# First layer's values with the input as the stationary operand, for two head pairs at a time, in a two-layer attention trunk

## What is computed

```python
qkv = (rms_norm(x, g0) @ w_qkv).reshape(s, 3, 16, 64)     # q, k, v
z = q @ k.T / 8                                           # per head
log_stay = where(strict, log_sigmoid(-z), 0)              # strict: key before query
log_a = log_sigmoid(z) + cumsum_from_right(log_stay shifted by one)
a = where(strict, exp(log_a), 0)
o = (a @ v) @ w_o
x = x + rms_norm(o, g1)
x = x + rms_norm(swiglu(rms_norm(x, g2), w_gate_up, w_down), g3)
```

## Time and profile before

| | |
|---|---|
| median of 3 runs | 778.37 us (777.60 to 779.53) |
| profiled execution, its own time | 777.7 us |
| its span | 775.8 us |
| TensorE matmul busy | 765.2 us, 99% of the span |
| VectorE busy | 507.3 us, 65% |
| ScalarE busy | 398.3 us, 51% |
| TensorE's granted clock | full in all 40 slices |
| DMA | 139.16 MB, mean 179 GB/s |

### The profile page before, as it was taken

How to read it: one execution, slowest core, us unless ns; L and a number is a source line. 1 busy time by engine, 2 the same in 40 slices (tenths; PEclk the granted TensorE clock), 3 DMA queues, 4 the chain that set the end, 5 groups by cost and what they waited for, 6 DMA issues and landing times.

```text
span 775.8 us, 12833 instructions
## 1 busy us (share of the span) xinstructions
PE 765.2 (99%) x4533; PEld 657.3 (85%) x4533; DVE 507.3 (65%) x688; ACT 398.3 (51%) x542; POOL 114.0 (15%) x173
## 2 busy tenths in 40 slices
PE   8999999999999999999999999999999999999996
PEld 7999977888888888998889898898888888888885
DVE  6888987675455455768767668577647654554543
ACT  5665666553343343855656656656546534433421
POOL 2000001200000000345425235143002000000000
PEclk9999999999999999999999999999999999999999
DMA  8534856675654554668785675685642855556502
GB/s 234 165 114 135 266 196 209 222 239 185 216 195 162 175 190 126 162 182 220 178 219 146 163 211 146 162 230 177 217 136 78 300 193 190 189 180 216 198 0 54
DMA packets 161537, 139.16 MB, mean 179 GB/s; under 512 B 6616, under 2 KB 151104, under 8 KB 161504
## 3 DMA queue, kind: packets, MB, share of 16 engines
q1 hardware_dynamic: 157536, 131.55, 54.7%
q0 software_dynamic: 3712, 6.88, 4.4%
q10 hardware_dynamic: 256, 0.30, 0.1%
HBM read 137.60 MB, written 1.11 MB: 179 GB/s over the span
## 4 chain that ended last, share of the span: by engine, by line
PE 93%; DVE 3%; issue 2%; ACT 2%; DVEq 0%; ACTq 0%; POOLq 0%; POOL 0%
PE ps L1149 20%; PE ps L1151 20%; PE ps L1150 20%; PE ps L1383 9%; PE ps L1385 5%; PE ps L1155 4%; PE ps L1156 4%; PE ps L1157 4%; PE ps L1440 1%; PE ps L1297 1%; PE ps L1449 1%; DVE w_lo L759 1%; PE ps L1226 1%; PE ps L1237 1%; PE ps L1204 1%
## 5 line engine op out<-in xcount | busy, mean ns | idle before, releaser
L759 DVE TENSOR_TENSOR w_lo<-raw,w_hi 128x2048 fp32r<-128x2048 f32 (+2 forms) x144 | 279.3, 1954 | 33.6 <-ACT w_hi L477 32.1
L477 ACT ACTIVATE w_hi<-raw 128x2048 fp32r<-128x2048 f32 (+2 forms) x144 | 232.3, 1636 | 50.6 <-DMA raw<-in_w_kv_b 24.0
L1149 PE MATMUL ps<-w_hi,xt 128*128 128x512 f32 x352 | 139.5, 396 | 0.0
L1151 PE MATMUL ps<-w_hi,xt 128*128 128x512 f32 x352 | 137.4, 390 | 0.0
L1150 PE MATMUL ps<-w_lo,xt 128*128 128x512 f32 x352 | 137.1, 389 | 0.0
L638 ACT ACTIVATE work<-ps,stat 128x256 f32<-128x256 f32 x44 | 20.9, 476 | 201.7 <-PE ps L1151 201.7
L1149 PE MATMUL ps<-w_hi,ot 128*128 128x512 f32 x240 | 94.9, 395 | 0.5 <-DVE w_lo L759 0.4
L1151 PE MATMUL ps<-w_hi,ot 128*128 128x512 f32 x240 | 93.5, 390 | 0.0
L1150 PE MATMUL ps<-w_lo,ot 128*128 128x512 f32 x240 | 93.4, 389 | 0.0
L1151 PEld LDWEIGHTS ps<-w_hi,xt 128*128 128x128 f32 x352 | 66.1, 188 | 14.0
L1149 PEld LDWEIGHTS ps<-w_hi,xt 128*128 128x128 f32 x352 | 66.1, 188 | 13.6 <-issue 0.6
(11 more groups left out here) (143 smaller groups left out, 1216.1 us busy)
## 6 DMA issues: line engine op xcount, KB each, us to landing
raw<-in_w_gate_up SPq DMA_DIRECT2D x88, 512.0 KB, 4.8
raw<-in_w_kv_b SPq DMA_DIRECT2D x96, 256.0 KB, 4.1
raw<-in_w_down SPq DMA_DIRECT2D x22, 1024.0 KB, 4.9
raw<-in_w_q_b SPq DMA_DIRECT2D x48, 256.0 KB, 4.1
raw<-in_w_qkv_a SPq DMA_DIRECT2D x23, 512.0 KB, 4.9
raw<-in_w_o_a SPq DMA_DIRECT2D x4, 1024.0 KB, 6.1
work<-bias_rows POOLq DMA_DIRECT2D x64, 64.0 KB, 3.1
raw<-in_w_o_b SPq DMA_DIRECT2D x4, 1024.0 KB, 4.9
```

Of the source, the lines that this page charges most:

```text
L477: act.activation(w_hi[:, s % CUT, 0:size(s)], raw[:, s % RAW, 0:size(s)], ACT.Copy).then_inc(hi_made, 1)
L759: dve.tensor_tensor(w_lo[:, c, 0:n], raw[:, s % RAW, 0:n], w_hi[:, c, 0:n].bitcast(F32), ALU.subtract).then_inc(lo_made, 1)
L1149: mm(out, xs[0], ws[0], start=start, stop=False)
L1151: return mm(out, xs[1], ws[0], start=False, stop=stop)
```

## The change

V of two pairs is now one product, with `xt` stationary (128 tokens at a time) and 256 columns of `w_v` moving. Its result has tokens on partitions. It is made in two halves of the contraction: half h is one unit (four of the eight blocks of features by 256 columns, again 512 KB), is worked on in step h-1, and the halves h (even) and h+1 add up in the same PSUM bank. ScalarE copies the bank out for both pairs after the second half, with the factor per token as its scale (two instructions of 128 x 256 for two pairs, instead of one for each). `turn_v`, `take_v_a` and the buffer `va_t` go.

The sequence of units changes: queries of pair p are unit 3p+1, keys 3p+2, half h of the values 3h. Pair 0 and the first halves stand at the start: units 0 and 1 are queries and keys of pair 0, unit 2 half 0, unit 3 half 1. So before step 1 TensorE runs 24 more matmuls, step p projects queries and keys of pair p and half p+1, and the last step has no V. The programs of ScalarE and VectorE cut unit 6 before step 1, and units 3p+4 to 3p+6 in step p (before 3p+3 to 3p+5). By this unit 24, the first of `w_o`, is the third unit of step 6 on both engines: ScalarE rounds it ahead of the Abs of pair 6, VectorE cuts it ahead of the outputs of pair 5 and the scores of pair 6. SyncE's order of DMAs stays that of the units.

```diff
@@ -158,8 +158,7 @@
 ka = carve(SEQ)
-va_t = carve(SEQ)
-va = carve(SEQ)
+va = carve(NT * 2 * P).rearrange("p (t n) -> p t n", t=NT)
 later = carve(P)
@@ -251,6 +250,14 @@
+def query_a(p):
+    return A0 + (3 * p + 1 if p else 0)
+def value_a(h):
+    return A0 + (3 * h if h else 2)
@@ -309,10 +316,19 @@
-    def pair_a(p, j, cs=range(3)):
+    def query_key_a(p, j, cs=range(2)):
         for c in cs:
-            load(A0 + 3 * p + c, j, lambda r: r.rearrange("p (k n) -> p k n", k=KT),
+            load(query_a(p) + c, j, lambda r: r.rearrange("p (k n) -> p k n", k=KT),
                  qkv_dram[:, c, :, ds(j * (2 * P) + p * P, P)])
+    def half_values_a(h, j):
+        k4, cols = slice(4 * (h % 2), 4 * (h % 2) + 4), ds(j * (2 * P) + h // 2 * (2 * P), 2 * P)
+        load(value_a(h), j, lambda r: r.rearrange("p (k n) -> p k n", k=4), qkv_dram[:, 2, k4, cols])
+    def step_a(p, j):
+        query_key_a(p, j)
+        half_values_a(p + 1, j)
@@ -346,16 +362,18 @@
     sp.dma_start(first[:, 4:8], qkv_dram[:, 0, 4:8, 0:P]).then_inc(landed[0], 16)
-    pair_a(0, 0, (1, 2))
+    query_key_a(0, 0, [1])
+    half_values_a(0, 0)
     sp.dma_start(ones[:, :], square[:, 3, :]).then_inc(ones_in, 16)
...
     sp.dma_start(strict, square[:, 2, :]).then_inc(strict_in, 16)
-    pair_a(1, 0)
+    half_values_a(1, 0)
     with sp.Fori(0, 3) as j:
-        pair_a(2, j)
-        pair_a(3, j)
+        step_a(1, j)
+        step_a(2, j)
+    query_key_a(PAIRS - 1, 0)
     sp.dma_start(mask_in, mask).then_inc(mask_in_s, 16)
@@ -547,10 +565,12 @@
         act.activation(ell, ell, ACT.Ln, bias=1.0).then_inc(ell_made, 1)
-        act.wait_ge(vt_done, j * 2 + a + 1)
-        if a >= 1:
-            act.wait_ge(pva_done, j * 2 + a)
-        act.activation(va, bank(2, 0, SEQ), ACT.Copy).then_inc(va_made, 1)
+        if a % 2 == 0:
+            act.wait_ge(w_used, j * 6 + value_a(a + 1) + 1)
+            act.wait_ge(*((pva_done, j * 2 + a) if a else (xrs_made, NT)))
+            for t in range(NT):
+                inst = act.activation(va[:, t, :], bank(2, 2 * P * t, 2 * P), ACT.Copy, scale=x_rs(0, t))
+            inst.then_inc(va_made, 1)
         act.wait_ge(spl_masked, j * 2 + a + 1)
@@ -687,7 +707,7 @@
     hi_half(1, 1)
-    for u in range(2, 6):
+    for u in range(2, 7):
         hi(A0 + u)
@@ -697,7 +717,7 @@
-        s = A0 + 3 * a + 6
+        s = A0 + 3 * a + 7
         attend_a(a, j, [lambda: (hi(s, j), hi(s + 1, j)), lambda: hi(s + 2, j)])
@@ -706,8 +726,8 @@
     step_a(PAIRS - 3, 0)
-    attend_a(PAIRS - 2, 0, [lambda: (hi(WOA0), hi(WOA0 + 1)), lambda: None])
-    attend_a(PAIRS - 1, 0, [lambda: (hi(WOA0 + 2), hi(WOA0 + 3)), lambda: (hi(FA0), hi(FA0 + 1))])
+    attend_a(PAIRS - 2, 0, [lambda: (hi(WOA0 + 1), hi(WOA0 + 2)), lambda: None])
+    attend_a(PAIRS - 1, 0, [lambda: hi(WOA0 + 3), lambda: (hi(FA0), hi(FA0 + 1))])
     boundary(0, WOA0 + 3, 2)
@@ -876,18 +896,12 @@
     def take_qk_a(p, j):
-        dve.wait_ge(w_used, j * 6 + A0 + 3 * p + 2)
+        dve.wait_ge(w_used, j * 6 + query_a(p) + 2)
         dve.scalar_tensor_tensor(qa, bank(0, 0, SEQ), SCALE, rows[:, :], ALU.mult, ALU.mult)
...
-    def take_v_a(p, j):
-        dve.wait_ge(w_used, j * 6 + A0 + 3 * p + 3)
-        if p >= 1:
-            dve.wait_ge(vt_done, j * 2 + p)
-        dve.tensor_tensor(va_t, bank(1, 0, SEQ), rows[:, :], ALU.mult).then_inc(vat_made, 1)
     def step_a(p, j):
-        s = A0 + 3 * p + 3
+        s = A0 + 3 * p + 4
         if p >= 2:
@@ -895,7 +909,6 @@
         mask_a(p - 1, j)
-        take_v_a(p, j)
         lo(s + 1, j)
@@ -1072,19 +1085,17 @@
     lo(A0 + 4)
-    take_v_a(0, 0)
     lo(A0 + 5)
+    lo(A0 + 6)
     dve.wait_ge(strict_in, 16)
     step_a(1, 0)
-    step_a(2, 0)
     with dve.Fori(0, 2) as j:
+        step_a(2, j)
         step_a(3, j)
-        step_a(4, j)
+    step_a(PAIRS - 2, 0)
     outputs_a(PAIRS - 3, 0)
...
     take_qk_a(PAIRS - 1, 0)
-    lo(WOA0)
-    take_v_a(PAIRS - 1, 0)
     stay_a(PAIRS - 2, 0)
@@ -1180,8 +1191,8 @@
-        s = A0 + 3 * p + c
-        halved = p == 0 and c < 2
+        s = query_a(p) + c
+        halved = p == 0
         if not halved:
@@ -1205,13 +1216,24 @@
-    def turn_v(a, j):
-        pe.wait_ge(vat_made, j * 2 + a + 1)
-        if a >= 1:
-            pe.wait_ge(va_made, j * 2 + a)
-        for t in range(NT):
-            inst = pe.transpose(bank(2, P * t, P), va_t[:, P * t:P * t + P], eye[:, :])
-        inst.then_inc(vt_done, 1)
+    def values_a(h, j, ks=range(4)):
+        s, half = value_a(h), h % 2
+        pe.wait_ge(lo_made, j * 6 + s + 1)
+        if h == 0:
+            pe.wait_ge(rows_made, 1)
+        elif not half:
+            pe.wait_ge(va_made, j + h // 2)
+        w = cut_unit(s, k=4)
+        for k in ks:
+            for t in range(NT):
+                out, xs = bank(2, 2 * P * t, 2 * P), [xt[:, n, 4 * half + k, P * t:P * t + P] for n in range(2)]
+                mm(out, xs[0], w[0][:, k, :], start=not half and k == 0 and t == 0, stop=False,
+                   skip_group_check=True)
+                mm(out, xs[0], w[1][:, k, :], start=False, stop=False, skip_group_check=True)
+                inst = mm(out, xs[1], w[0][:, k, :], start=False, stop=half == 1 and k == 3, skip_group_check=True)
+        if k == 3:
+            inst.then_inc(w_used, 1)
@@ -1228,15 +1250,16 @@
     def outputs_a(a, j):
-        pe.wait_ge(va_made, j * 2 + a + 1)
+        pe.wait_ge(va_made, j + a // 2 + 1)
         if a >= 1:
...
             out = ps[DH * hh:DH * hh + DH, 7 * 512:7 * 512 + SEQ]
-            mm(out, va[:, DH * hh:DH * hh + DH], wts[:, hh, 0:SEQ], start=True, stop=False,
+            v = P * (a % 2) + DH * hh
+            mm(out, va[:, 0, v:v + DH], wts[:, hh, 0:SEQ], start=True, stop=False,
                skip_group_check=True)
-            inst = mm(out[:, P:SEQ], va[:, P + DH * hh:P + DH * hh + DH], wts[:, hh, SEQ:WA],
+            inst = mm(out[:, P:SEQ], va[:, 1, v:v + DH], wts[:, hh, SEQ:WA],
                       start=False, stop=True, skip_group_check=True)
@@ -1245,12 +1268,11 @@
             outputs_a(p - 2, j)
-        turn_v(p - 1, j)
         project_a(p, j, 0, 0, 0)
         project_a(p, j, 1, 0, SEQ)
-        project_a(p, j, 2, 1, 0, range(2))
+        values_a(p + 1, j, [0])
         sums_a(p - 1, j)
-        project_a(p, j, 2, 1, 0, range(2, KT))
+        values_a(p + 1, j, [1, 2, 3])
@@ -1503,7 +1525,8 @@
        start=True, stop=True).then_inc(bias_done, 1)
-    project_a(0, 0, 2, 1, 0)
+    values_a(0, 0)
+    values_a(1, 0)
     pe.wait_ge(bias_out_made, 1)
@@ -1514,17 +1537,14 @@
     outputs_a(last - 2, 0)
-    turn_v(last - 1, 0)
     project_a(last, 0, 0, 0, 0)
     project_a(last, 0, 1, 0, SEQ)
-    project_a(last, 0, 2, 1, 0)
     sums_a(last - 1, 0)
     scores_a(last, 0)
-    turn_v(last, 0)
     out_proj(WOA0, 0, 0, [0, 1, 2])
...
     out_proj(WOA0, 0, 0, [3])
-    pe.wait_ge(va_made, PAIRS)
+    pe.wait_ge(va_made, PAIRS // 2)
     out_proj(WOA0, 0, 1, [0, 1])
```

More of the change, by code:

```diff
@@ L233, in build @@
         ot_hi, ot_made = sem("ot_hi"), sem("ot_made")
-        z_done, vt_done, r_done, pva_done = (sem(n) for n in ("z_done", "vt_done", "r_done", "pva_done"))
-        qka_made, vat_made, va_made, abs_made, exp_made, ell_made = (sem(n) for n in (
-            "qka_made", "vat_made", "va_made", "abs_made", "exp_made", "ell_made"))
+        z_done, r_done, pva_done = (sem(n) for n in ("z_done", "r_done", "pva_done"))
+        qka_made, va_made, abs_made, exp_made, ell_made = (sem(n) for n in (
+            "qka_made", "va_made", "abs_made", "exp_made", "ell_made"))
         spl_made, spl_masked, spl_hi, spl_cut_made, arg_made, stay_made, wts_made, wts_masked = (sem(n) for n in (
```

## The result

| | before | after |
|---|---|---|
| median of 6 runs each | 778.32 us (777.60 to 779.53) | 784.97 us (784.63 to 786.47) |
| ratio | | 1.0089, 95% interval 1.0078 to 1.0099 |
| profiled execution, own time | 777.7 us | 784.9 us |
| its span | 775.8 us | 783.2 us |
| TensorE matmul busy | 765.2 us | 766.8 us |

The change made the kernel 6.7 us slower. The forecast was +1.9 us, with a range up to 782.4 us.

A forecast was written before the change was run, and what follows sets the result against it. TensorE was taken to bound the steps, VectorE the output projection's last weights. T's +1.7, +1.0 + L to VectorE's scores of pair 6, and -2.8 after them gave +1.9 us: 780.3 us, range 777.0 to 782.4.

The forecast's parts named there:

- T: Start of the scores of pair 6: 2.9 us later for one more unit, six transpose pairs earlier, +1.7 us.
- L: At the attention's end, the time from the start of pair 6's scores to unit 24's landing: 2.0 us.
- No stall in a step: In the attention's steps, ScalarE's two copies of V stay covered and the sums are ready in time: no cost.
- The margin: Before a step's sums: their input is ready 0.9 us before TensorE wants it, enough for being wanted 0.2 earlier.
- Step 2 of the end: Before the Abs of pair 6: unit 24 lands behind x at 91.45, 2.0 us after the scores start.
- The bound from the last DMA of x: In SyncE's queue: x lands 8.0 us after issue and unit 24 2.65 behind it, so +4.2 us.
- the slower rival: Before the Abs of pair 6: ScalarE waits longer for unit 24, +4.2 us, 782.6 us; chance 0.20.
- Step 4: VectorE's way from the scores of pair 6 to pair 7: -2.5 us; TensorE stalls 2.9 before pair 6's sums.
- step 5: From pair 7's scores to the first matmul on unit 27: VectorE nearly all in a row, -0.3 us.
- the third rival: The same as the slower rival: unit 24 later still at the Abs of pair 6, 782.6 us; chance 0.20.
- that TensorE sets the end: At the attention's end: unit 24 in time, VectorE has slack, all eight transpose pairs count, -1.6 us; chance 0.15.
- that VectorE sets it with unit 24 in time: At the attention's end: unit 24 lands in time and VectorE's work decides, -0.3 down to -1.3 us; chance 0.20.

The follow-up runs named there:

- the gap filled: The changed kernel with 11 matmuls into an unused bank ahead of the sums of pair 6, where TensorE idled: 782.55 us, ratio 1.0057.
- the best version: Changed kernel, units 24 and 25 loaded before mask and x, unit 24 handled later, scores of pair 6 earlier, VectorE's steps written out: 777.98 us, ratio 0.9996.

## Why the prediction was wrong

The mechanism and its place were right: unit 24 moved ahead of the Abs of pair 6, ScalarE waits for it, VectorE and TensorE after it. Its sizes were not. In the profiled execution the first matmul on unit 27 came 7.5 us later, not 1.9:

| term | forecast | measured |
|---|---|---|
| T, start of the scores of pair 6 | +1.7 | +2.7 (92.30 - 89.57 in TensorE's timelines) |
| L, unit 24 after T | 2.0 | 4.1 (96.44 - 92.30) |
| from unit 24 to the first matmul on unit 27 | 24.65 | 27.1 (123.58 - 96.44) |

- *Transposes, 0.20 us a pair*: right. 0.21 by doubling them, 0.18 by the length of a step. The 275 ns that the Trainium skill (TensorE: Matmul & The Clock Gate, Part 4: PE-mode transpose) gives for each don't show as a cost here.
- *V's products at 0.12 us, 24 for each pair*: right, L1231, L1233 and L1234 start 0.12 us apart.
- *"No stall in a step"*: wrong, 0.8 us of T. The margin was read from step 3 alone. In step 2 the table load had already used it up, so the sums of pair 1 wait 0.2 us. Another 0.5 is VectorE's late start in the same step, which went away with its loop. The start kept another 0.2.
- *Step 2 of the end, L*: wrong by a factor of two, and it is worth 2.1 us. The rate was right, the order was not. I had let the transfers follow one another, x through before unit 24 begins and nothing else beside it. The sum had x through 0.6 us before T, which is 91.66 here, with 2.49 MB moved. So much had been moved (start and end, length, busy times, clock, DMA share, GB/s):

```profile
81.00:91.66 10.66, 10.66 (x90) 10.13 (x91) 9.10 (x15) 6.34 (x8) 0.00 (x0) 1.00 0.86 237
81.00:96.44 15.44, 15.44 (x130) 14.34 (x131) 11.65 (x17) 6.90 (x8) 0.00 (x0) 1.00 0.91 274
```

  That is 2.5 MB. But the last DMA of x, issued at 85.77, took 8.1 us and landed at 93.9, and unit 24 at 96.44, 10.0 us after its issue. By then 4.2 MB had been moved. Units 22 to 24, mask and x are 3.5 MB; the other 0.7 MB can only be of units 25 and 26, whose loads went out at 92.50 and 94.24. At the 391 GB/s of 92.5 to 96.4 us they are worth 1.8 us, an estimate. The bound from the last DMA of x gave L = 4.3, and I set it aside as the slower rival; it was the better row, since it measured a landing in that very queue. That unit 24 can't overtake x was true; that a load in front is served first was not: issued ahead of x it took 9.5 us. The Trainium skill (DMA: Bandwidth & Descriptors, Queues, rings and completion order) also says that completion is not first in, first out for an issuing engine, and that half of it is the one which this case bears out.
- *Step 4, "a stall of 2.9 us" on TensorE*: the stall was 4.95 us, longer by just the 2.1 us of L, and the sum had no term for what it does to the clock. That was the largest miss, 2.4 us. It also broke step 5, where VectorE was to be busy in a row: it waited 2.21 us for TensorE's slow sums. The Trainium skill (TensorE: Matmul & The Clock Gate, HAM oscillation) describes this very thing, a wait for a DMA between matmuls after which the next ones run at half clock; the trace after agrees (0.50 from 106 to 110), and I hadn't weighed it. With the gap filled, the third term was 24.4 us, near the 24.65 of the forecast. The whole was then 782.55 us, where the third rival had 782.6 with L = 4.3. That agreement is partly luck: with the measured T of +2.7 and the L of that run, 96.67 - 92.87 = 3.8, the sum gives 783.1.
- *The rivals*: that TensorE sets the end, and that VectorE sets it with unit 24 in time, both need the unit in time. With it cut late the second one's order of things holds: 779.28, the same as the kernel before, where -0.3 was forecast and 1.0 us was lost in T.
- *Nothing is given back later*: right, 659.6 us against 659.7.

The 1.6 us of the transposes never came through in any version, and where they went is shown only in part: 0.2 us at the start, 0.5 at VectorE's late start in step 2, and at the end 1.4 us of TensorE's waits for VectorE in the best version, against 0.4 before. That version, 777.98 us, isn't clear of the kernel before.

## What to carry to other kernels

When a change shifts a sequence of prefetched units by one, look where the sequence changes its unit: a larger one that moves one slot forward lands ahead of work it had never stood before. Price such a load by the landing of a neighbour in the same queue, not by bytes over a rate in the order of issue, and count what is issued behind it. And a stall of several microseconds on TensorE can cost more than its length, here 2.4 us beyond its 4.95: add the half-speed matmuls behind it, and what waits for them.

## What was not expected of the hardware

- A 1 MB load issued with 1.4 MB behind it took 9.5 us to land, one with the same 1.4 MB in front of it 10.0. In these two profiles later transfers of the queue slowed an earlier one nearly as much as the other way round.
- After 4.95 us without a matmul TensorE worked at its lower clock from 104.98 to about 111.1 us, where the distance of the 512-column matmuls goes from 0.43 back to 0.23.
- VectorE began an operation 0.5 us late in the first pass of the changed kernel's loop, and not when the same steps were written out. In the first pass of the loop of the kernel before it did not. The cause stays open.
